# Routing by row halves before the experts of a two-block layer

## The reference, cut to what matters

```python
logits = (hf @ w_router) + b_router              # hf = rmsnorm(x, g_ffn), 256 x 1024
top_vals, top_idx = lax.top_k(logits, 4)
top_w = softmax(top_vals)
# for each chosen (token, expert):
gu = xb @ w_gate_up[e] + b_gate_up[e]            # 1024 -> 2 x 1024
g, u = min(gu[:, :1024], 7), clip(gu[:, 1024:], -7, 7)
y = ((u + 1) * g * sigmoid(1.702 * g)) @ w_down[e] + b_down[e]
x = x + sum over the token's experts of top_w * y
x = x + sigmoid(rmsnorm(x, g_ple) @ w_ple_gate) * (p @ w_ple_proj)
```

## Time and profile before

| | |
|---|---|
| timed runs | median 1385.06 us of three, 1383.64 to 1385.48 |
| profiled execution | span 1381.8 us from the first to the last instruction; the page gives no other time for it |
| PE busy | 1313.6 us, 95% of the span, 6736 matmul records |
| PE weight loads | 689.4 us, 50% |
| DVE, ACT, POOL busy | 497.1, 313.6, 54.0 us |
| transfers | 498.75 MB, mean 361 GB/s |

### The profile page before, as it was taken

The page is one execution under the profiler, slowest core; times in us unless marked ns, Lnnn a source line. Parts: engine busy times, 40 slices in busy tenths (PEclk is TensorE's granted clock), DMA queues, the critical chain, the costliest instruction groups (busy, mean ns, idle before and its releaser), DMA issues.

```text
span 1381.8 us, 16681 instructions
## 1 busy us (share of the span) xinstructions
PE 1313.6 (95%) x6736; PEld 689.4 (50%) x6736; DVE 497.1 (36%) x741; ACT 313.6 (23%) x437; POOL 54.0 (4%) x70
## 2 busy tenths in 40 slices
PE   9999999999999989999899998999989899999998
PEld 5656586433343334333333333333333346898997
DVE  3676474222222212221222112221222127766764
ACT  4375553101011001010110101010110015633631
POOL 2122110000000000000000000000000001000000
PEclk9999999999999999999999999999999999999999
DMA  9998677999999999999999999999999998446430
GB/s 328 387 333 291 216 292 312 419 429 428 428 428 428 428 429 428 429 428 429 428 429 429 429 429 429 428 428 428 429 428 428 429 425 316 136 173 209 162 125 31
DMA packets 77264, 498.75 MB, mean 361 GB/s; under 512 B 7127, under 2 KB 8618, under 8 KB 52650
## 3 DMA queue, kind: packets, MB, share of 16 engines
q1 hardware_dynamic: 76090, 496.06, 87.8%
q0 software_dynamic: 704, 2.10, 0.5%
q10 hardware_dynamic: 432, 0.07, 0.0%
HBM read 497.06 MB, written 1.05 MB: 360 GB/s over the span
## 4 chain that ended last, share of the span: by engine, by line
PE 65%; DMA 31%; DVE 2%; ACT 1%; issue 1%; POOL 0%; SPq 0%; DVEq 0%; POOLq 0%; ACTq 0%
PE ps L1925 28%; DMA ring<-in_w_gate_up_dram 15%; DMA arena<-in_w_gate_up_dram 13%; PE ps L1638 5%; PE ps L1640 5%; PE ps L1639 5%; PE ps L1919 3%; PE ps L1913 3%; DMA ring<-in_w_down_dram 3%; PE ps L1659 2%; PE ps L1660 2%; PE ps L1665 2%; PE ps L1675 1%; PE ps L2115 1%; PE ps L1652 1%; PE ps L2040 1%
## 5 line engine op out<-in xcount | busy, mean ns | idle before, releaser
L1925 PE MATMUL ps<-ring,arena 128*64 128x512 f32 x2304 | 518.2, 597 | 47.5 <-DMA ring<-in_w_down_dram 24.2
L1925 PEld LDWEIGHTS ps<-ring,arena 128*64 128x64 f32 x2304 | 158.0, 137 | 370.4 <-issue 292.7
L1925 PE MATMUL ps<-arena 128*64 128x512 f32 x768 | 172.9, 598 | 4.0 <-DMA arena<-in_w_gate_up_dram 3.8
L1353 DVE TENSOR_SCALAR arena<-ps 128x512 f32<-128x512 f32 x32 | 22.1, 691 | 351.2 <-PE ps L1925 351.2
L818 ACT ACTIVATE arena<-arena 128x512 f32<-128x512 f32 x32 | 20.1, 630 | 400.6 <-DVE arena L1353 400.6
L1925 PEld LDWEIGHTS ps<-arena 128*64 128x64 f32 x768 | 51.5, 137 | 113.2 <-issue 93.9
L1332 DVE COPY arena<-ps 64x512 f32<-64x512 f32 x32 | 22.0, 689 | 199.4 <-PE ps L1925 199.4
L1327 DVE TENSOR_TENSOR X<-X,ps 128x1024 f32<-128x1024 f32 x34 | 41.4, 1217 | 136.0 <-PE ps L1919 136.0
L1640 PE MATMUL ps<-arena_highs,w_low 128*128 128x256 f32 x320 | 89.8, 281 | 0.0
L827 ACT COPY arena<-ps 64x512 f32<-64x512 f32 x32 | 18.5, 580 | 261.4 <-PE ps L1925 261.4
L1919 PE MATMUL ps<-arena 128*128 128x512 f32 x136 | 67.1, 617 | 0.0
(11 more groups left out here) (317 smaller groups left out, 1569.9 us busy)
## 6 DMA issues: line engine op xcount, KB each, us to landing
ring<-in_w_gate_up_dram SPq DMA_DIRECT2D x96, 2048.0 KB, 33.4
ring<-in_w_down_dram SPq DMA_DIRECT2D x48, 2048.0 KB, 35.2
arena<-in_w_gate_up_dram SPq DMA_DIRECT2D x32, 2048.0 KB, 34.0
ring<-in_w_in_dram SPq DMA_DIRECT2D x38, 1024.0 KB, 7.0
arena<-in_w_down_dram SPq DMA_DIRECT2D x16, 2048.0 KB, 34.7
ring<-in_w_ada_dram SPq DMA_DIRECT2D x24, 1024.0 KB, 14.1
ring<-in_w_out_dram SPq DMA_DIRECT2D x12, 1024.0 KB, 5.8
ring<-in_w_ple_gate_dram SPq DMA_DIRECT2D x4, 1024.0 KB, 29.7
```

Source lines behind the costliest of these rows:

```text
L1925: last = T.matmul(ps[at:at + CAP, bank, :], lhsT, w(g), start=False, stop=stop)
```

## The change

- The sum of x is taken per half and 512 columns (`x_sum(h, g)`). The chunk parts `(o1, 0)` and `(o1, 1)` change places in the order of splits, and the first four output products are in the order (0,0), (1,0), (0,1), (1,1). The sum of squares of the second half is taken in two pieces.
- The transposes of the second half of x come in two groups of four, one ahead of `route(0)` and one behind it.
- `choose` makes the mask in another way: the four smaller of the eight largest values are overwritten by a large number, `match_replace` replaces the others in a copy of the logits, and where copy and logits differ is the mask. `lg` has four more columns for it.
- Positions are computed per half, and so is the one-hot of the first two experts (`pick_first`). PE gathers the first half's terms as soon as it can, around the second half's counts, and then the second half's.
- The embedding products move into the last two pairs of experts, between the second expert's first product and the first expert's second product; ACT copies 1024 columns there. The last pass of the expert loop is written out on PE, the last two on ACT.
- SP fills bin 7 right behind bin 2.

```diff
                 load(0, k)
                 if k == 4:
                     ada_moved(1)
+                if k == 2:
+                    load(0, BINS - 1)
             sp.wait_ge(s["chunk_used1"], used1("o1"))
-            load(0, BINS - 1)
             load(0, GROUPS - 1)
...
+            def choose(h):
+                run(V.memset(top_v[:, h, TOPK:8], -NEG))
+                join()
+                run(V.match_replace(rest[:, h, :], top_v[:, h, :], lg[:, h, :], NEG))
+                join()
+                V.tensor_tensor(mask[:, h, :], lg[:, h, 0:E], rest[:, h, 0:E], ALU.not_equal).then_inc(s["mask_done"], 1)
+
+            def pick_first(h):
+                dve.wait_ge(s["pos_full"], h + 1)
+                dve.wait_ge(s["mask_done"], h + 1)
+                run(V.scalar_tensor_tensor(posm[:, h, 0:E], ps[:, POS_BANK[h], 0:E], 1.0, mask[:, h, :],
+                                           ALU.add, ALU.mult))
+                join()
+                both = [P, 2, CAP]
+                V.tensor_tensor(pick[:, h], slots.rearrange("p (e n) -> p e n", e=2),
+                                posm[:, h, 0:2].unsqueeze(2).to_broadcast(both), ALU.is_equal
+                                ).then_inc(s["pick_ready"], 1)
...
-            x_sum(0)
+            x_sum(0, 0)
+            x_sum(0, 1)
+            dve.wait_ge(s["x_half"], 1)
+            join()
             mean_of_x(0)
+            x_sum(1, 0)
             columns_of_x()
             power_of_x(0)
-            x_sum(1)
-            choose(0, lambda: mean_of_x(1))
+            x_sum(1, 1)
+            mean_of_x(1)
+            best(0)
+            choose(0)
+            largest(0)
             power_of_x(1)
-            choose(1, lambda: None)
...
+            best(1)
+            pick_first(0)
+            choose(1)
+            largest(1)
+            pick_first(1)
...
-            def columns_of_x(h):
-                pe.wait_ge(s["x_half"], h + 1)
+            def columns_of_x(h, j):
                 p = free(pe, f"fT{h}")
-                for k in range(KC):
+                for k in range(4 * j, 4 * j + 4):
                     last = T.transpose(flat(p, P, k * P), X[:, h, k * P:k * P + P], ident)
-                last.then_inc(full1[p], 1)
+                return last
...
             out_product(1, 1, (1,))
+            moved(pe, "o0")
+            columns_of_x(1, 0).then_inc(full1[U1["fT1"][0]], 1)
             route(0)
-            columns_of_x(1)
-            pe.wait_ge(s["proj_in"], 48)
-            pe.wait_ge(s["p_moved"], 1)
-            embedding(0)
+            moved(pe, "o1")
+            columns_of_x(1, 1).then_inc(full1[U1["fT1"][0]], 1)
             route(1)
             pe.wait_ge(s["mask_done"], 1)
-            count(0, before, 0)
-            count(E, ones, 0)
-            count(2 * E, ones, 0)
-            embedding(1)
-            pe.wait_ge(s["mask_done"], 2)
-            count(E, before, 1)
-            count(2 * E, ones, 1).then_inc(s["pos_full"], 1)
+            count(0, 0, before, 0, True, True).then_inc(s["pos_full"], 1)
+            count(1, 0, ones, 0, True, False)
+            count(1, E, ones, 0, False, False)
...
-            embedding(2)
-            pe.wait_ge(s["tok_ready"], HALVES)
+            pe.wait_ge(s["tok_ready"], 1)
+            pe.wait_ge(s["p_moved"], 1)
             pe.wait_ge(s["pick_ready"], 1)
-            gather(0).then_inc(s["gather_half"], 1)
-            gather(1).then_inc(s["gather_done"], 1)
+            for k in range(4):
+                gather_term(k, 0)
+            pe.wait_ge(s["mask_done"], 2)
+            count(1, 0, before, 1, False, True)
+            count(1, E, ones, 1, False, True).then_inc(s["pos_full"], 1)
+            for k in range(4, KC):
+                gather_term(k, 0)
+            pe.wait_ge(s["tok_ready"], 2)
+            pe.wait_ge(s["pick_ready"], 2)
+            for k in range(KC):
+                last = gather_term(k, 1)
+                if k % 4 == 3:
+                    last.then_inc(s["gather_done" if k // 4 else "gather_half"], 1)
...
+                def embedding(h):
+                    pe.wait_ge(s["proj_in"], 48)
+                    pe.wait_ge(s["pT_kept"], 1)
+                    for g in range(2):
+                        for k in range(2):
+                            last = T.matmul(ps[:, 6 + g, :], pT_kept[h][:, k, :], w_emb[:, k, g * 512:g * 512 + 512],
+                                            start=k == 0, stop=k == 1)
+                    last.then_inc(s["p_full"], 1)
...
                 gather(0)
                 gate_and_up(1, first_hidden_columns)
+                if embedded is not None:
+                    pe.wait_ge(s["sc_used"], i * 2 + (2 + FIRST))
+                    embedding(embedded)
                 down(0)
...
+            with pe.Fori(0, extra * QUADS + (QUADS - 1)) as i:
+                quad(i)
+            quad(extra * QUADS + (QUADS - 1), (0, 1))
             pe.wait_ge(s["hidT_ready"], extra * E + (E + FIRST))
-            embedding_term(3, 0, pT_last)
+            keep_busy(4, 1)
+            pe.wait_ge(s["p_moved"], 1 + HALVES)
```

More of the change, by code:

```diff
@@ L787, in _, with scaled_tokens @@
             act.wait_ge(s["p_full"], 1)
[L788 to L798, removed]
+            columns_of_p = ps[:, 2, :].rearrange("p (a b) -> p a b", a=2)
+            A.copy(pT_kept[0], columns_of_p[:, :, 0:P])
+            A.copy(pT_second, columns_of_p[:, :, P:S]).then_inc(s["p_moved"], 1)
+            def scaled_tokens(h):
                 act.wait_ge(s["pow_out"], FFN_NORM + h)
@@ L835, in _ @@
                 sigmoid(1)
+                if h is not None:
+                    embedded(h)
                 result(0)
@@ L838, in _ @@
                 result(1)
+            with act.Fori(0, extra * PAIRS + (PAIRS - HALVES)) as i:
+                pair_of_experts(i)
+            for h in range(HALVES):
+                pair_of_experts(extra * PAIRS + (PAIRS - HALVES + h), h)
             def w_split(m):
@@ L1196, in x_sum @@
                 else:
[L1197 to L1206, removed]
+                    dve.wait_ge(s["chunk_used1"], used1(f"o{g}"))
+                part = X[:, h, g * 512:g * 512 + 512]
+                ins = V.tensor_tensor(part, part, ps[:, 2 * b + h, :], ALU.add)
                 if h:
-                    moved(dve, "o0")
-                    moved(dve, "o1")
-                    dve.sem_inc(s["x_half"], 1)
-                else:
-                    dve.wait_ge(s["x_half"], 1)
-                    join()
+                    ins.then_inc(moved1[b], 1)
+                elif g:
+                    ins.then_inc(s["x_half"], 1)
+                else:
+                    run(ins)
             def columns_of_x():
@@ L1234, in choose @@
                 join()
-                V.tensor_scalar(st[:, 4 + h:5 + h], top_v[:, h, 0:1], -1.0, None, ALU.mult).then_inc(s["lg_ready"], 1)
[L1236 to L1252, removed]
@@ L1317, in _ @@
             gathered(1)
+            for r in range(1, ROUNDS):
+                run(V.tensor_scalar(posm[:, :, r * E:r * E + E], posm[:, :, 0:E], -1.0 * CAP * r, None, ALU.add))
             for h in range(HALVES):
@@ L1863, in route, with count @@
                 for k in range(KC):
-                    last = T.matmul(ps[:, RT_BANK[h], h * E:h * E + E], HT[:, k, h * P:h * P + P], wr[:, k, :],
+                    last = T.matmul(ps[:, RT_BANK[h], 0:E], HT[:, k, h * P:h * P + P], wr[:, k, :],
                                     start=k == 0, stop=k == KC - 1)
                 last.then_inc(s["rt_full"], 1)
-            def count(n, half, h):
-                return T.matmul(ps[:, POS_BANK, n:n + E], half, mask[:, h, :], start=h == n == 0, stop=h == 1 or n == 0,
+            def count(bank, n, of, h, first, last):
+                return T.matmul(ps[:, POS_BANK[bank], n:n + E], of, mask[:, h, :], start=first, stop=last,
                                 skip_group_check=True)
-            def embedding_term(n, k, columns):
-                bank, g, h = EMB[n]
-                return T.matmul(ps[:, bank, :], columns[:, k, :], w_emb[:, k, g * 512:g * 512 + 512],
-                                start=k == 0, stop=k == 1, skip_group_check=True)
-            def embedding(n):
-                h = EMB[n][2]
-                for k in range(2):
-                    last = embedding_term(n, k, pT[:, :, h * P:h * P + P])
-                last.then_inc(s["p_full"], 1)
             for h in range(HALVES):
-                for g in range(2):
-                    out_product(h, g, (0,))
-                if not h:
-                    columns_of_merged(1)
+                out_product(h, 0, (0,))
+            out_product(0, 1, (0,))
+            columns_of_merged(1)
+            out_product(1, 1, (0,))
             pe.wait_ge(s["p_in"], 16)
@@ L1912, in gather @@
                     for h in range(HALVES):
-                        last = T.matmul(ps[:, 2 + j, k % 4 * P:k % 4 * P + P], tok[:, h, k, :],
```

(4 more changed lines are left out.)

125 lines of the change are left out of this document (72 added, 53 removed).

## The result

| | kernel before | changed kernel |
|---|---|---|
| median of 20 runs each | 1385.14 us (1383.32 to 1387.22) | 1387.62 us (1385.94 to 1389.48) |
| ratio, 95% interval | | 1.0016 [1.0010, 1.0022] |
| profiled span | 1381.8 us | 1384.9 us |
| mean granted clock of an execution | 0.998 (mean of 33 executions, in the comparison of the first experiments) | 0.995 (mean of the 20) |

Forecast was 1383.8 us, 1.3 us faster, with a range up to 1386.2. The change makes the kernel 2.5 us slower, outside the range and on the other side. In every execution whose span is listed the time lies 1.74 to 1.89 us above the span.

A forecast was written before the change was run, and what follows sets the result against it. Expert weights over DMA set the pace, their end moving with PE's first use of a bin; PE sets the end. Routing -2.7 plus last pair +1.4 gives -1.3 us: span 1380.5, plus remainder 3.3, 1383.8 us; range 1381.5 to 1386.2.

The forecast's parts named there:

- the first sentence on the clock: Granted clock is 1.00 in every profiled stretch asked for of the kernel before, so no clock step enters the sums.
- the wait for `o1`: PE before the second half's transposes: waits for output product o1's PSUM pair, 0.85 us paid back for the removed product.
- handovers to DVE: Routing, between PE's logits and DVE's choice: 0.12 us counted for the handover.
- Routing, -2.7 us: From logits to first expert: first expert at 229.3 instead of 232.04 us, 2.7 us earlier; bounds 1.5 to 3.2.
- the register read: PE reads the number of extra rounds between gather and bias rows: 0 to 1.26 us exposed, 0.5 taken.
- Embedding products in the last pair, +1.4 us: Ahead of the last pair's first down product: 3.43 us against 2.05 us of waiting, 1.4 us later; bounds 0 to 3.4.
- Bin 7 sooner, nothing: Weight stream before the experts: bin 7 fills the first hole, 4.9 us; worth nothing by itself, only cover.
- the cover: Bin 7 sooner; without it the stream could take no more than 3.5 to 4 us of a faster routing.
- The stream's end moves with the first use and by nothing else: Expert weight stream runs unbroken from 259 us, so its end moves by as much as PE's first use of a bin.
- The sum, -1.3 us: Whole kernel: -2.7 + 1.4 = -1.3 us against the profiled span of 1381.8, so 1380.5.
- The remainder of 3.3 us: Median of the runs, 1385.06 us, lies 3.3 us above the profiled span; kept unchanged, giving 1383.8 us.
- (c): Rival: last quad's new code arrives late on PE, one 4.9 us wait, +3.6 us, 1388.7 us; chance 9%.

The follow-up runs named there:

- again: The changed kernel once more, unchanged: 1387.46 us, ratio 1.0012 to the kernel before.
- filler: The changed kernel plus three 512-column matmuls that nothing reads, one in each of PE's three routing gaps: 1383.42 us, ratio 0.9986 to the kernel before.
- fill4: The changed kernel plus three filler matmuls in the routing and two in PE's 2.53 us gap near 164 us: 1382.73 us, ratio 0.9982 to the kernel before.
- late7: `fill4` with bin 7 issued behind the wait for the last output product again, as before the change: 1382.88 us, ratio 0.9984 to the kernel before.
- befill: The kernel before plus only two filler matmuls in PE's 2.53 us gap near 164 us: 1384.22 us, ratio 0.9993 to the kernel before.
- best2: `best` with the second half's transposes in PSUM pair 1, no first filler, the next two in bank 5: 1381.17 us, ratio 0.9967 to the kernel before.
- best: `fill4` with both embedding products in the pair before the last, around its first down product: 1381.75 us, ratio 0.9977 to the kernel before.
- before2: The kernel before, unchanged, profiled once more: 1385.69 us, span 1383.9 us.

## Why the prediction was wrong

The step that failed is the first sentence on the clock: the granted clock is 1.00 in every stretch asked for, "so no clock step enters below". That row told of the kernel before, where PE had no gap in the routing because embedding products stood in the waits. The prediction took them out as work, 1.72 and 1.80 us, and never asked what PE would do instead: 0.85 of the wait for `o1` was in its own sum, as idle time. Its handovers to DVE were gaps too. What the runs showed in its place: the clock at 0.50 for 6.8 us behind those gaps. The cost is 4.0 us in the medians (`again` against `filler`). In the profile of the changed kernel 2.8 us of it can be read: 15.48 us of routing against 12.67. The rest isn't assigned; the fall's length differs between executions, and one profile need not show the median's.

The Trainium skill ("TensorE: Matmul & The Clock Gate", section "A second HAM failure mode: psum-queue depth-cycling") tells of a kernel in which PE was idle for short times between groups of matmuls often enough that the clock went back and forth between its levels. The three gaps of 0.94, 0.72 and 0.63 us agree with it. It would have been a rival with the right sign.

The other steps, at a steady clock:

- *Routing, -2.7 us.* Right once the gaps are filled: 15.32 to 12.66. `fill4` reaches the first expert at 229.00, forecast 229.3, from output products that end 0.3 us earlier than the forecast's. The transposes waited for `o1` as said. Loading the values and replacing took 0.09 + 0.18 us, forecast 0.26; the one-hot of 128 elements 0.29, forecast 0.32. Only the register read differs: of the 0.5 us nothing shows, since the bias rows start right behind the gather.
- *Embedding products in the last pair, +1.4 us.* Right in kind, too large: the tail grew by 0.96 us, and moving the product out of the last pair gave back 1.0.
- *Bin 7 sooner, nothing.* Right (`late7`). The routing's gain of 2.65 stayed below the 3.5 us from which the cover would matter.
- *The stream's end moves with the first use and by nothing else.* Nearly: its way from first issue to last landing is 905.3 to 906.1 us in the profiles with the old order of refills (`late7` the shortest, `befill` the longest) and 905.9 to 906.8 in those with bin 7 sooner. The ranges overlap, and the medians of `late7` and `fill4` are 0.15 us apart, so what the new order costs here is open.
- *The sum, -1.3 us.* Borne out where the clock is kept, as far as the noise allows: 1.3 us (`late7` and `befill`, one chip), 1.5 (`fill4` and `befill`), 2.3 (`filler` and the kernel before on its chip). These kernels hold fillers that the forecast did not have. On that last chip the 2.3 us gained and the 4.0 us for the clock make the +1.8 of `again`; the first comparison gave +2.5. That the sum came so close is in part luck, since the tail was put 0.4 us too high.
- *The remainder of 3.3 us* between span and median was no constant: time lies 1.8 us above the span of the same execution, and the profiled execution was the fastest of its three, without the fall at 168. It did not cause the miss, but the sum stood on an execution whose time, about 1383.6 us, lies 1.5 us below the median.
- *Rivals.* (c), slower by late code, is refuted: four fetches more (30 against 26), and PE's two waits in the last quad (0.86 and 0.64 us) are for bins. The slower outcome came from a case that was not listed.

## What to carry to other kernels

When work is taken out of PE's waits, list the gaps that open and ask what the granted clock does next; a clock that is 1.00 in the profile of before may stand on the very instructions that are removed. Compare two orders of work at one clock (fill the gaps of both with matmuls that nothing reads) before pricing them. A wait that can be taken away instead of filled may give more: the routing of `best2` is 1.07 us shorter than that of `fill4`. And a product moved to the end of a stream belongs where the stream, not PE, still sets the pace (`best`).

## What was not expected of the hardware

- The clock fell behind gaps of 0.63 to 0.94 us with PE busy for 5.34 of 7.00 us around them, 128x128 and 128x32 products between. One such gap behind other work (0.61 to 0.62 us near 166 in `fill4`, `befill` and `best2`) brought no fall.
- The falls in the routing were 3.4, 6.8, 10.2 and 13.7 us long, different for the same kernel (6.8 and 3.4 in the two profiles of the changed one, where they start 0.01 and 0.8 us after the third gap began). The same gap of 2.53 us was followed by a fall in one profile of the kernel before and by none in the other.
- At the lower level a gather pass took 0.18 us from start to start (4.41 for 24) instead of 0.12 (2.80 for 24), and a matmul of 512 columns near 171 us in `before2` 0.42 to 0.43 instead of 0.23.
- Mean granted clock and time go together: about 1 us for 0.001 over the runs of the changed kernel.
